# Ten weight slots as one ring in the order of use, and expert passes unrolled by five

## What is computed

```python
def expert_block(args):
    e, tok, wt = args
    xb = h_pad[tok]
    gu = xb @ w_gu[e] + b_gu[e]
    gate = jnp.minimum(gu[:, :D_FF], SWIGLU_LIMIT)
    up = jnp.clip(gu[:, D_FF:], -SWIGLU_LIMIT, SWIGLU_LIMIT)
    act = (up + 1.0) * gate * jax.nn.sigmoid(SWIGLU_ALPHA * gate)
    y = act @ w_down[e] + b_down[e]
    return y * wt[:, None].astype(y.dtype)
```

## Time and profile before

| | us |
|---|---|
| median of 3 runs (1187.72 to 1189.18) | 1188.93 |
| profiled execution, its time | 1188.63 |
| its span, first to last instruction | 1186.7 |
| PE busy | 1130.4 (95%) |
| DVE busy | 459.9 (39%) |
| weight queue q1, share of the 16 DMA engines | 92.9% |

### The profile page before, as it was taken

The page is one execution under the profiler, slowest core; times in us unless marked ns, Lnnn a source line. Parts: engine busy times, 40 slices in busy tenths (PEclk is TensorE's granted clock), DMA queues, the critical chain, the costliest instruction groups (busy, mean ns, idle before and its releaser), DMA issues.

```text
span 1186.7 us, 17539 instructions
## 1 busy us (share of the span) xinstructions
PE 1130.4 (95%) x7007; PEld 499.8 (42%) x7007; DVE 459.9 (39%) x959; ACT 136.7 (12%) x304; POOL 110.6 (9%) x142
## 2 busy tenths in 40 slices
PE   6989999999999999999999999999999999999996
PEld 5866778653333333333333333333333333333331
DVE  5898767544222222233222223222222222222223
ACT  3212223041000000000000000000000000000002
POOL 2867750000000000000000000000000000000000
PEclk9999999999999999999999999999999999999998
DMA  9992369988999999999999999999999999999995
GB/s 347 321 338 103 107 223 387 416 337 340 427 430 427 430 426 430 426 431 426 431 426 431 426 389 427 430 428 429 427 430 427 429 428 428 429 429 428 429 425 206
DMA packets 56124, 459.96 MB, mean 388 GB/s; under 512 B 10216, under 2 KB 10432, under 8 KB 27936
## 3 DMA queue, kind: packets, MB, share of 16 engines
q1 hardware_dynamic: 54944, 458.46, 92.9%
q10 hardware_dynamic: 1152, 1.12, 0.3%
HBM read 458.51 MB, written 1.05 MB: 387 GB/s over the span
## 4 chain that ended last, share of the span: by engine, by line
PE 64%; DMA 27%; DVE 6%; ACT 1%; issue 1%; SPq 1%; DVEq 0%; ACTq 0%
PE ps L1010 23%; PE ps L1052 15%; DMA ring<-in_w_gu 13%; DMA ring<-in_w_down 13%; PE ps L586 6%; PE ps L985 3%; PE ps L929 3%; PE ps L782 2%; PE ps L1032 2%; PE ps L800 2%; PE ps L879 1%; PE ps L765 1%; PE ps L850 1%; DMA ring<-in_w_ada 1%; PE ps L1040 1%
## 5 line engine op out<-in xcount | busy, mean ns | idle before, releaser
L1052 PE MATMUL ps<-ring,tmp 128*64 128x512 f32 x1024 | 228.1, 595 | 17.6 <-ACT tmp L1262 8.9
L1010 PE MATMUL ps<-ring,zone 128*64 128x512 f32 x1024 | 228.8, 596 | 9.8 <-DMA ring<-in_w_gu 8.7
L1010 PE MATMUL ps<-zone 128*64 128x512 f32 x1024 | 227.0, 595 | 0.1
L1759 DVE TENSOR_TENSOR x_tok<-x_tok,ps 128x512 f32<-128x512 f32 x128 | 82.0, 682 | 262.4 <-PE ps L985 258.7
L1052 PEld LDWEIGHTS ps<-ring,tmp 128*64 128x64 f32 x1024 | 80.8, 137 | 144.2 <-issue 128.5
L1010 PEld LDWEIGHTS ps<-ring,zone 128*64 128x64 f32 x1024 | 69.9, 137 | 164.4 <-issue 140.2
L1010 PEld LDWEIGHTS ps<-zone 128*64 128x64 f32 x1024 | 70.3, 137 | 153.1 <-issue 147.9
L1259 ACT ACTIVATE hT<-hT 128x256 f32<-128x256 f32 x64 | 23.9, 417 | 739.8 <-DVE hT L1774 739.8
L586 PE MATMUL ps<-hT,ring 128*128 128x256 f32 x448 | 103.0, 387 | 1.5 <-DVE hT L1426 1.5
L1774 DVE TENSOR_SCALAR hT<-ps 128x256 f32<-128x256 f32 x64 | 24.2, 419 | 191.9 <-PE ps L1010 191.9
L586 PEld LDWEIGHTS ps<-hT,ring 128*128 128x128 f32 x448 | 84.7, 193 | 15.9 <-issue 4.3
(11 more groups left out here) (322 smaller groups left out, 837.6 us busy)
## 6 DMA issues: line engine op xcount, KB each, us to landing
ring<-in_w_down SPq DMA_DIRECT2D x61, 2048.0 KB, 21.1
zone<-in_w_gu SPq DMA_DIRECT2D x60, 2048.0 KB, 24.6
ring<-in_w_gu SPq DMA_DIRECT2D x59, 2048.0 KB, 27.9
ring<-in_w_ada SPq DMA_DIRECT2D x24, 1024.0 KB, 13.0
ring<-in_w_in SPq DMA_DIRECT2D x16, 1024.0 KB, 14.2
ring<-in_w_gu SPq DMA_DIRECT2D x10, 1024.0 KB, 9.4
zone<-in_w_gu SPq DMA_DIRECT2D x8, 1024.0 KB, 13.8
ring<-in_w_down SPq DMA_DIRECT2D x6, 1024.0 KB, 17.5
```

The source lines that it names most:

```text
L1010: last = mm(ps[CAP * h:CAP * h + CAP, b, :], hg[:, 2 * j + kk, :], w[:, kk, D * b + 512 * h:D * b + 512 * h + 512], start=False, stop=(j = ...
L1052: last = mm(ps[CAP * h:CAP * h + CAP, 3, :], actT[:, q, j, :], w[:, q, 512 * h:512 * h + 512], start=False, stop=(j == DN_PIECES - 1 and q ...
L1759: V.tensor_tensor(x_tok[:, t, 512 * h:512 * h + 512], x_tok[:, t, 512 * h:512 * h + 512], ps[:, bank + h, :], ALU.add).then_inc(S["comb_ad ...
```

## The change

The ten places become one ring in the order of use: piece k of all (six per pass) goes to place k modulo 10, gate/up or down alike, and waits for the use of piece k-10. The semaphores of the places become `piece_in[0..9]`. SP's program has one order throughout: down of expert 1, then gate/up and down of each expert in turn. Since 10 places and 6 pieces per pass come round together after five passes (30 pieces, three laps), the loops on SP and on PE are unrolled by five: SP has one loop of five turns and four passes written out; PE has a loop of six turns of five passes. ACT, DVE and POOL are unchanged.

```diff
-    gu_slots = [qkov, bcxs, pair(PRE - 12), pair(PRE - 10), ecos_at, merged_yb, pair(PRE - 4), pair(PRE - 2)]
-    dn_slots = [pair(PRE - 8), pair(PRE - 6)]
+    PIECES = 10
+    FIVE = 5
+    piece_slots = [qkov, bcxs, pair(PRE - 12), pair(PRE - 10), pair(PRE - 8), pair(PRE - 6),
+                   ecos_at, merged_yb, pair(PRE - 4), pair(PRE - 2)]
...
-            def next_gu(i, e, par):
+            def next_gu(i, e, k):
                 for j in range(GU_PIECES):
-                    sp.wait_ge(w_used, i * PASS + (USED - 2 * PASS + j + 1))
-                    load_gu(e, par, j)
-
-            def next_dn(i, e):
+                    sp.wait_ge(w_used, i * PASS + (USED - PIECES + j + 1))
+                    load_gu(e, k + j, j)
+
+            def next_dn(i, e, k):
                 for j in range(DN_PIECES):
-                    sp.wait_ge(w_used, i * PASS + (USED - PASS + GU_PIECES + j + 1))
-                    load_dn(e, j)
-
-            with sp.Fori(1, AHEAD) as q:
-                next_gu(2 * q, 2 * q, 0)
-                next_dn(2 * q - 1, 2 * q - 1)
-                next_gu(2 * q + 1, 2 * q + 1, 1)
-                next_dn(2 * q, 2 * q)
-            with sp.Fori(AHEAD, EXPERTS // 2 - 1) as q:
-                next_dn(2 * q - 1, 2 * q - 1)
-                next_gu(2 * q, 2 * q, 0)
-                next_dn(2 * q, 2 * q)
-                next_gu(2 * q + 1, 2 * q + 1, 1)
+                    sp.wait_ge(w_used, i * PASS + (USED - PIECES + GU_PIECES + j + 1))
+                    load_dn(e, k + GU_PIECES + j, j)
+
+            next_dn(1, 1, PASS)
+            with sp.Fori(0, (EXPERTS - 2) // FIVE - 1) as q:
+                for u in range(FIVE):
+                    next_gu(FIVE * q + (2 + u), FIVE * q + (2 + u), PASS * (2 + u))
+                    next_dn(FIVE * q + (2 + u), FIVE * q + (2 + u), PASS * (2 + u))
+            z = EXPERTS - 1
+            for e in range(EXPERTS - FIVE, z):
+                next_gu(e, e, PASS * e)
+                next_dn(e, e, PASS * e)
...
-                    pe.wait_ge(gu_in[GU_PIECES * par + j], turn * 16 + 16)
-                    w = gu_slot(par, j)
+                    pe.wait_ge(piece_in[(k + j) % PIECES], landed(j))
+                    w = gu_slot(k + j)
...
-            item(0, 0, 1, first=True)
+            item(0, 0, 0, first=True)
             item_table()
-            with pe.Fori(0, EXPERTS // 2 - 1) as q:
-                item(2 * q + 1, 1, q + 1)
-                item(2 * q + 2, 0, q + 2)
-            item(EXPERTS - 1, 1, EXPERTS // 2, last_expert=True)
+            with pe.Fori(0, (EXPERTS - 2) // FIVE) as q:
+                for u in range(FIVE):
+                    item(FIVE * q + (1 + u), 3 * q, PASS * (1 + u))
+            item(EXPERTS - 1, 0, PASS * (EXPERTS - 1), last_expert=True)
```

More of the change, by code:

```diff
@@ L237, in build @@
     arrived = [sem(f"arrived{s}") for s in range(SLOTS)]
-    gu_in = [sem(f"gu_in{s}") for s in range(2 * 4)]
-    dn_in = [sem(f"dn_in{s}") for s in range(2)]
+    piece_in = [sem(f"piece_in{s}") for s in range(10)]
     w_used = sem("w_used")
@@ L341, in build @@
     PASS = GU_PIECES + DN_PIECES
-    AHEAD = 8
     def held(n):
@@ L350, in pair, with gu_slot, dn_slot @@
         return ring[:, n % SLOTS:n % SLOTS + 2, :].rearrange("p s n -> p (s n)")
-    gu_slots = [qkov, bcxs, pair(PRE - 12), pair(PRE - 10), ecos_at, merged_yb, pair(PRE - 4), pair(PRE - 2)]
-    dn_slots = [pair(PRE - 8), pair(PRE - 6)]
[L355 to L359, removed]
+    PIECES = 10
+    FIVE = 5
+    piece_slots = [qkov, bcxs, pair(PRE - 12), pair(PRE - 10), pair(PRE - 8), pair(PRE - 6),
+                   ecos_at, merged_yb, pair(PRE - 4), pair(PRE - 2)]
+    def gu_slot(k):
+        return piece_slots[k % PIECES].rearrange("p (k n) -> p k n", k=2)
+    def dn_slot(k):
+        return piece_slots[k % PIECES].rearrange("p (k n) -> p k n", k=4)
     def slot(n, k):
@@ L391, in dn_rows, with load_gu, load_dn @@
                 return w_down[0, bass.ds(e, 1)].rearrange("e (h p q) n -> p (e h) q n", h=2, p=P)
[L393 to L397, removed]
+            def load_gu(e, k, j):
+                sp.dma_start(gu_slot(k), gu_rows(e)[:, j]).then_inc(piece_in[k % PIECES], 16)
+            def load_dn(e, k, j):
+                sp.dma_start(dn_slot(k), dn_rows(e)[:, j]).then_inc(piece_in[k % PIECES], 16)
             def half_gu(e, j, b):
-                sp.dma_start(gu_slot(e, j)[:, b:b + 1, :], gu_rows(e)[:, j, b:b + 1]).then_inc(gu_in[GU_PIECES * e + j], 16)
+                k = PASS * e + j
+                sp.dma_start(gu_slot(k)[:, b:b + 1, :], gu_rows(e)[:, j, b:b + 1]).then_inc(piece_in[k], 16)
             def half_dn(j, b):
-                sp.dma_start(dn_slot(j)[:, 2 * b:2 * b + 2, :], dn_rows(0)[:, j, 2 * b:2 * b + 2]).then_inc(dn_in[j], 16)
+                k = GU_PIECES + j
+                sp.dma_start(dn_slot(k)[:, 2 * b:2 * b + 2, :], dn_rows(0)[:, j, 2 * b:2 * b + 2]).then_inc(piece_in[k], 16)
             for n in range(place["in", 3] + 1):
@@ L459, in last_gu @@
             def last_gu(e, j, b, s):
-                sp.dma_start(gu_slot(1, j)[:, b:b + 1, :], gu_rows(e)[:, j, b:b + 1]).then_inc(s, 16)
+                k = PASS * e + j
+                sp.dma_start(gu_slot(k)[:, b:b + 1, :], gu_rows(e)[:, j, b:b + 1]).then_inc(s, 16)
             def last_dn(e, j, b, s):
[L463 to L467, removed]
@@ L468, in _ @@
-            next_dn(z - 1, z - 1)
+                k = PASS * e + GU_PIECES + j
+                sp.dma_start(dn_slot(k)[:, 2 * b:2 * b + 2, :], dn_rows(e)[:, j, 2 * b:2 * b + 2]).then_inc(s, 16)
             for j in range(GU_PIECES):
-                sp.wait_ge(w_used, z * PASS + (USED - 2 * PASS + j + 1))
+                k = PASS * z + j
+                sp.wait_ge(w_used, USED + k - PIECES + 1)
                 if j < GU_PIECES - 1:
-                    load_gu(z, 1, j)
+                    load_gu(z, k, j)
@@ L473, in _ @@
                 else:
-                    last_gu(z, j, 0, gu_in[GU_PIECES + j]), last_gu(z, j, 1, last_gu_in)
+                    last_gu(z, j, 0, piece_in[k % PIECES]), last_gu(z, j, 1, last_gu_in)
             for j in range(DN_PIECES):
-                sp.wait_ge(w_used, z * PASS + (USED - PASS + GU_PIECES + j + 1))
+                k = PASS * z + GU_PIECES + j
+                sp.wait_ge(w_used, USED + k - PIECES + 1)
                 if j < DN_PIECES - 1:
-                    load_dn(z, j)
+                    load_dn(z, k, j)
@@ L479, in _ @@
                 else:
-                    last_dn(z, j, 0, dn_in[j]), last_dn(z, j, 1, last_dn_in)
+                    last_dn(z, j, 0, piece_in[k % PIECES]), last_dn(z, j, 1, last_dn_in)
             sp.wait_ge(S["item_sb"], 5)
@@ L483, in _ @@
             with sp.If(count > EXPERTS):
[L484 to L489, removed]
+                with sp.Fori(0, OVER // FIVE) as q:
+                    for u in range(FIVE):
+                        with sp.If(FIVE * q + (EXPERTS + u) < count):
+                            e = sp.value_load(itab[0:1, bass.ds(FIVE * q + (EXPERTS + u), 1)], min_val=0, max_val=EXPERTS - 1)
+                            next_gu(FIVE * q + (EXPERTS + u), e, PASS * (EXPERTS + u))
+                            next_dn(FIVE * q + (EXPERTS + u), e, PASS * (EXPERTS + u))
             for i in range(TT):
@@ L985, in combine, with item, landed @@
                     mm(ps[:, 6 + h, :], pickwT[half, P * t:P * t + P], ysb[half, :], start=True, stop=True).then_inc(S["comb_up"], 1)
-            def item(i, par, turn, first=False, last_expert=False):
+            def item(i, lap, k, first=False, last_expert=False):
+                def landed(j):
+                    return lap * 16 + (16 * ((k + j) // PIECES) + 32)
                 if first:
@@ L1043, in item @@
                 for j in range(DN_PIECES):
-                    pe.wait_ge(dn_in[j], i * 16 + 32)
-                    w = dn_slot(j)
+                    pe.wait_ge(piece_in[(k + GU_PIECES + j) % PIECES], landed(GU_PIECES + j))
+                    w = dn_slot(k + GU_PIECES + j)
                     for q in range(4):
@@ L1066, in _ @@
                 gather()
[L1067 to L1070, removed]
+                with pe.Fori(0, OVER // FIVE) as q:
+                    for u in range(FIVE):
+                        with pe.If(FIVE * q + (EXPERTS + u) < count):
+                            item(FIVE * q + (EXPERTS + u), 3 * q, PASS * (EXPERTS + u))
             pe.wait_ge(S["y_sb"], count)
```

## The result

The changed kernel takes 1193.39 us (median of 8 runs, 1191.24 to 1194.57), the kernel before beside it 1187.21 us (median of 8, 1185.46 to 1190.35). The ratio is 1.0047, 95% interval 1.0035 to 1.0059: slower by half a per cent, where 1187.6 and a range up to 1190.5 were forecast. The profiled execution took 1194.57 us, 5.9 us more than that of before.

A forecast was written before the change was run, and what follows sets the result against it. The weight stream was taken as the bound. Against the profiled 1188.63 us: -3.0 (hole) + 0.2 (first fetch) + 1.5 (fetches at five turns) = -1.3, so 1187.3; median 0.3 above the profiled time, forecast 1187.6 us, range 1185.4 to 1190.5.

The forecast's parts named there:

- The bound: From about 265 us to the last landing the weight stream sets the end, 29.36 us per pass against PE's 27.70.
- PE's 20 us to spare: Over 30 passes PE could be 20 us faster than the stream; it spends this waiting for pieces, at no cost.
- Its own sign of being wrong: The forecast counted itself wrong if PE sat idle more than 3 us at the turns of its loop.
- The hole: Stream dip at 660 to 720 us, from four down pieces in a row on SP; closing it gains 3.0 us.
- What waits instead: Down pieces issue up to 20 us earlier, gate/up up to two pieces later; PE waits in some ten last passes; cost 0.
- SP's longer loop: Same instructions per piece on SP, any delay of an issue covered by the backlog: cost 0.
- the thin backlog near 290 us: Near 290 us the backlog covering SP's issue delays is thin, about one piece or 5 us.
- Rival 3: The hole does not close or another opens, 1 to 3 us of stream go again: 1188.5 to 1190; chance 0.13.
- The loop does not stay: PE's 6.9-packet loop is fetched again at five turns, 40 packets: 1.5 us, after 0.2 us for the first fetch.
- Rival 2: PE's turns become the bound, above 7.7 us per turn; 1196.6 at 9.5 us per turn; chance 0.12.
- The chances of the three classes: Against the kernel before, with about 0.2% as no change: faster 0.23, same 0.62, slower 0.15.
- The price of a packet: Each 16 KB code packet costs the weight stream 0.038 us, or 0.064 us by its own duration; the lower was taken.

The follow-up runs named there:

- written out: The changed kernel with PE's 30 middle passes written out, no loop and no turn back: ratio 1.0032 to the kernel before.
- the shortened changed kernel: The changed kernel computing one of the gather's three partial products, PE's loop 5.6 packets of code: ratio 0.9973 to the kernel before.
- the switch at another place: The kernel before with SP's change from first to second order four turns later (AHEAD 12 instead of 8): ratio 1.0004.
- the ring of nine: The changed kernel with nine places as one ring from piece 6 on and loops of three passes: ratio 0.9992 to the kernel before.
- the loop of six: The kernel before with only PE's loop unrolled to six passes, 8.3 packets of code: ratio 1.0096.
- the loop of four: The kernel before with only PE's loop unrolled to four passes (5.5 packets of code) and two more passes written out: ratio 1.0007.
- the loop of 6.3 packets: The changed kernel computing two of the gather's three partial products: ratio 1.0002 to the kernel before.

## Why the prediction was wrong

**The bound: right.** The weight stream sets the end before and after; PE's 20 us to spare are real. The changed kernel lost 14.0 on missing instructions and some 4 on the slower clock behind them, without any effect on the end: written out, without these stalls, it was no faster than its fewer code packets explain (below). Some of that is luck. The text had 17 us to spare for the turns and allowed at most "slight idle"; it knew nothing of the clock, and 18 us are about all there was. The stream, longer than forecast, left PE more time. Its own sign of being wrong, more than 3 us of idle at the turns, came true over the five of them, though not as the cause of the loss.

**The hole: right in cause and size.** -3.0 us was the term. The two late landings of before make 2.8 us, the shortened changed kernel's stream is 2.8 us shorter than that of before (889.0 for 891.7), and the switch at another place moved it.

**What waits instead, SP's longer loop, the thin backlog near 290 us: right**, no new dip. PE waited for gate/up pieces only, as forecast, but five times in all, since the turns had used up its lead. Rival 3 did not happen here, but the ring of nine shows how near it was: one use more to wait for, and 2.8 us were lost there.

**The loop does not stay: right**, 68 packets for "about 60": nine per turn where the text had eight, three close behind the branch and then one every 20 us or so, not in a burst. The turn was dearer than in the text, 6.2 us for 3.54, of which the sequencer's lead covered about 4.2; the first two turns lost 1.6 and 1.9 us more at a second fetch. Rival 2 had the direction of that right and put the threshold at 7.7 us per turn. The chances of the three classes do not add up as written: the parts named for "slower" give 0.13 (0.02 + 0.11), not 0.15, and those for "same" 0.64, not 0.62.

**The price of a packet: this step failed.** The text said: "16 KB at 428.5 GB/s are 0.038 us; by its own duration [...] 1.0 us on one of 16 engines, 0.064 us", and took the lower, 1.5 us for 40 packets. Both values spread a packet's cost over all 16 engines. The runs show it stays on the engine that carries it, only eight engines fall behind, and a piece waits for the slowest. One packet holds its engine back by about 1.55 us, the step in which the lags grow; so n packets more, dealt out evenly over eight engines, cost n x 1.55 / 8 = 0.194 n us, three to five times my price. For the changed kernel that is 49 x 0.194 = 9.5, less the hole 2.8: +6.7 us; the stream is 6.7 us longer. Written out: 38 x 0.194 - 2.8 = +4.6; measured +4.7. The 1.55 and the eight were read from the changed kernel's own landings, so its sum shows only that they add up; the written-out kernel is the independent test. For the loop of six the sum gives 9.7 (the hole stays) and the stream is 11.3 us longer. There the lag was paid twice over, once at the hole, where it was evened out (4.4 us grown until then, and the hole 2.3 us wider), and again from there to the end (5 us), which makes 11.7; why the hole widens was not tried. For few packets the rule is too low, because whole steps fall on one engine: 1.8 us for six (the loop of four), 3.9 us for nine (the loop of 6.3 packets).

The evidence that I had taken for the lower price, 428 GB/s with two packets and 429 without, could not show it: a lag on a few engines is not a loss of rate while the others have backlog. It turns into time only where all engines must meet, at the landing of the pieces that gate PE and at the last one.

The rule that I had quoted from the Trainium skill, "Runtime: NRT & Kernel Launch", section "Instruction fetch mechanics", says also that crossing a block border costs "one DMA tail-bump, mostly hidden". PE's side agrees: written out, it fetched 57 packets and never waited for one in the passes. The stream's side does not: 4.7 us longer. Of its two sizes, the two-block window is refuted again by the loop of 5.5 packets, which turned back six times in 0.22 to 0.25 us; the room of 2048 instructions, eight blocks, is compatible with 5.6 staying and 6.9 not if one or two blocks are taken by what is read ahead, and no run here separates these.

## What to carry to other kernels

Where all DMA engines are busy with one stream, code fetched by an engine's sequencer is part of that stream, and here it fell on half of the DMA engines, unevenly: count the packets on the instruction queues, and compare the first and the last of a transfer's 16 landings, before unrolling. Choose a ring's length so that it comes round in few passes: here nine places and three passes (4.2 packets of code) beat ten places and five passes (6.9), though a place is given up. And when a share seems to cost little on average over 16 engines, ask what it costs on the one that carries it.

## What the runs showed of the hardware that was not expected

- Code packets of 16 KB, with a median duration of 1.07 us in the changed kernel, set the engine that carries them back by about 1.55 us, and only 8 of the 16 engines fell behind: after 68 packets the last piece's landings were 11.9 us apart, after 57 9.9, after 31 6.2, after 18 to 25 1.8 to 3.3. After 69 in the loop of six they were 6.7 apart, since the hole had evened them out on the way. Why 1.55 and not 1.07, and why eight, stays open.
- PE's loop of 5.6 packets turned in 0.22 to 0.25 us every time, those of 6.9 and 8.3 never did (5.9 to 6.5 us each turn), and one of 6.3 turned four times in 0.22 to 0.25 us and once in 7.5 us, with runs spread over 6.8 us.
- Idles of PE of 2.1 to 2.3 us at three turns of the changed kernel were each followed by 3.4 us at a granted clock of 0.5; those of 1.6 to 2.0 us at its first two turns were not. In the loop of six one of 1.7 us was, and one of 2.1 us was not. What decides it stays open.
- A turn back to code that was not there took the sequencer 5.9 to 7.5 us under the full stream; the forward branch near the end, with the stream over, took 3.4 to 4.6 us.
